# Bonus row sums in four column tiles, spread over partitions by a transfer through DRAM, and one weight tile's low part written in two halves

## The reference, cut to what matters

```
z = h @ w_in[l]
...
bonus = jnp.sum(rh * kh * r_k.astype(f32), axis=-1, keepdims=True) * vh
y = (y + bonus.reshape(B, T, RWKV_DIM)) * g.astype(f32)
```

## Time and profile before

| | us |
|---|---|
| median of 3 runs | 1086.53 (1085.99 to 1086.6) |
| the profiled execution | 1085.98 |
| its span, first to last instruction | 1084.4 |
| TensorE (PE) busy | 1068.5 |
| VectorE (DVE) busy | 670.7 |
| ScalarE (ACT) busy | 535.0 |
| GpSimd (POOL) busy | 109.3 |

### The profile page before, as it was taken

The page is one execution under the profiler, slowest core; times in us unless marked ns, Lnnn a source line. Parts: engine busy times, 40 slices in busy tenths (PEclk is TensorE's granted clock), DMA queues, the critical chain, the costliest instruction groups (busy, mean ns, idle before and its releaser), DMA issues.

```text
span 1084.4 us, 17833 instructions
## 1 busy us (share of the span) xinstructions
PE 1068.5 (99%) x6584; PEld 856.5 (79%) x6584; DVE 670.7 (62%) x1159; ACT 535.0 (49%) x1060; POOL 109.3 (10%) x164
## 2 busy tenths in 40 slices
PE   8999999999999999999999999999999999999997
PEld 7887888767787787787877888888888888888886
DVE  4224655687887887878765445557677777742124
ACT  6426675635545555555554334555555556531122
POOL 8100000220120220212110010100000000000000
PEclk9999999999999999999999999999999999999999
DMA  7633333321220312314133453423333332322221
GB/s 199 156 89 88 92 85 86 92 60 40 50 49 31 88 44 66 69 60 122 55 118 99 141 151 113 136 79 97 96 97 97 97 96 79 99 95 97 97 78 77
DMA packets 155190, 99.16 MB, mean 91 GB/s; under 512 B 31033, under 2 KB 143975, under 8 KB 155127
## 3 DMA queue, kind: packets, MB, share of 16 engines
q1 hardware_dynamic: 148800, 79.72, 25.5%
q0 software_dynamic: 6176, 18.53, 7.0%
q10 hardware_dynamic: 151, 0.04, 0.0%
HBM read 89.81 MB, written 8.45 MB: 91 GB/s over the span
## 4 chain that ended last, share of the span: by engine, by line
PE 95%; DVE 2%; ACT 1%; issue 1%; DMA 1%; SPq 0%; DVEq 0%; ACTq 0%
PE ps L1711 16%; PE ps L1714 16%; PE ps L1713 16%; PE ps L1667 5%; PE ps L1669 4%; PE ps L1668 4%; PE ps L2196 4%; PE ps L2197 4%; PE ps L2195 4%; PE ps L1829 3%; PE ps L1785 1%; PE ps L1981 1%; PE ps L1909 1%; PE ps L1960 1%; PE ps L1954 1%; PE ps L1886 1%
## 5 line engine op out<-in xcount | busy, mean ns | idle before, releaser
L1152 DVE TENSOR_TENSOR wlo<-raw,whi 128x1024 fp32r<-128x1024 f32 x142 | 173.7, 1223 | 213.6 <-ACT whi L729 141.5
L729 ACT ACTIVATE whi<-raw 128x1024 fp32r<-128x1024 f32 x124 | 131.1, 1057 | 124.6 <-PE ps L1714 120.8
L1711 PE MATMUL ps<-xnh,whi 128*128 128x512 f32 x344 | 135.8, 395 | 0.0
L1714 PE MATMUL ps<-xnh,wlo 128*128 128x512 f32 x344 | 135.7, 395 | 0.0
L1713 PE MATMUL ps<-xnl,whi 128*128 128x512 f32 x344 | 135.7, 395 | 0.0
L1711 PE MATMUL ps<-xh,whi 128*128 128x512 f32 x248 | 99.7, 402 | 1.5 <-DVE xl L1170 1.5
L1714 PE MATMUL ps<-xh,wlo 128*128 128x512 f32 x248 | 97.9, 395 | 0.0
L1713 PE MATMUL ps<-xl,whi 128*128 128x512 f32 x248 | 97.8, 395 | 0.0
L1667 PE MATMUL ps<-xh,whi 128*128 128x512 f32 x184 | 87.4, 475 | 0.4 <-DVE wlo L1152 0.4
L1711 PEld LDWEIGHTS ps<-xnh,whi 128*128 128x128 f32 x344 | 64.8, 188 | 15.2
L1713 PEld LDWEIGHTS ps<-xnl,whi 128*128 128x128 f32 x344 | 64.8, 188 | 15.1
(11 more groups left out here) (345 smaller groups left out, 2238.0 us busy)
## 6 DMA issues: line engine op xcount, KB each, us to landing
raw<-in_w_in SPq DMA_DIRECT2D x108, 256.0 KB, 3.3
raw<-in_w_up SPq DMA_DIRECT2D x88, 256.0 KB, 3.2
raw<-in_w_down SPq DMA_DIRECT2D x44, 256.0 KB, 2.9
gates_scratch<-gst POOLq DMA_DIRECT2D x16, 256.0 KB, 2.6
raw<-in_w_proj_b SPq DMA_DIRECT2D x16, 256.0 KB, 4.1
raw<-in_w_proj_a SPq DMA_DIRECT2D x16, 256.0 KB, 3.2
gl<-gates_scratch POOLq DMA_DIRECT2D x16, 256.0 KB, 3.1
raw<-in_w_out SPq DMA_DIRECT2D x16, 256.0 KB, 3.1
```

The source lines that it names most:

```text
L729: act.activation(flat(whi[:, hb]), flat(raw[:, b]), ACT.Copy).then_inc(w_hi, 1)
L1152: dve.tensor_tensor(flat(lo[:, hb]), flat(raw[:, b]), flat(hi[:, hb]).bitcast(F32), ALU.subtract).then_inc(w_lo, 1)
L1711: pe.matmul(ps[bank][:, :], whi[:, hb, k, :], hi(k), start=first and k == 0, stop=False)
L1714: ins = pe.matmul(ps[bank][:, :], wlo[:, hb, k, :], hi(k), start=False, stop=last and k == kn - 1)
```

## The change

1. `bonus` becomes `bonus_rows` for pairs 0 to 6: four products with 32 stationary columns (`rkcols`: the two head columns scaled by r_k) and 128 moving columns each, writing four groups of 32 partitions of bank 5. ScalarE copies the 128x128 result to `brow` between `ktok`'s copy and the turned output's (`bonus_sums`), and makes `rkcols` (128x32) in place of `rkones` (128x128).
2. GpSimd, behind `remainder(n)` and ahead of `key_norms_in(n+1)`, stores `brow` to DRAM, waits for that to land, and issues two transfers that read one row for each head back into 64 partitions of `z[:, d+8]` (`bonus_back`).
3. VectorE's `add_bonus` waits for these transfers and multiplies two tiles of SBUF; it moves from behind level 2 to behind level 3, and `with_bonus` from behind level 3 to behind level 5, ahead of `gated`.
4. The low part of weight tile 3n+1 was written at the start of `invert`, in one instruction. It is now written in two halves, behind level 1 and behind level 2. TensorE waits for the first half ahead of the tile's k = 0 and for the second ahead of k = 4.

```diff
@@ gpsimd
+            def bonus_back(d):
+                pool.wait_ge(brow_ready, d + 1)
+                pool.dma_start(bonus_rows, brow[:, :]).then_inc(brow_stored, 16)
+                pool.wait_ge(brow_stored, 16 * (d + 1))
+                for h in range(2):
+                    pool.dma_start(z[h * HD:(h + 1) * HD, d + 8, :]
+                                   .rearrange("p (j t) -> p j t", j=NT),
+                                   by_head(bonus_rows, h)).then_inc(bonus_in, 16)
...
                 remainder(n)
+                bonus_back(n - 1)
                 if n < PAIRS - 1:
                     pool.wait_ge(yturn_ps, n)
                     key_norms_in(n + 1)
@@ scalar
+            def bonus_sums(d):
+                act.wait_ge(bsum_ps, d + 1)
+                act.activation(brow[:, :], ps[5][:, 0:P], ACT.Copy).then_inc(brow_ready, 1)
...
                     if lv == 2:
-                        act.activation(rkones[:, :], headones[:, :], ACT.Copy, scale=pcol("rk", n))\
+                        dst, src = (rkcols, keycols[:, KEY0:KEY0 + P // NT]) if following else \
+                            (rkones, headones[:, :])
+                        act.activation(dst[:, :], src, ACT.Copy, scale=pcol("rk", n))\
...
                 token_copies(n)
+                bonus_sums(n - 1)
                 turned_output(n - 1)
@@ vector
             def add_bonus(d):
-                dve.wait_ge(bonus_ps, d + 1)
-                dst, bank = (tile(d + 8), 5) if d < PAIRS - 1 else (bp[:, :], 2)
-                chain(dve.tensor_tensor(dst, tile(d + 16), ps[bank][:, :], ALU.mult))
+                if d < PAIRS - 1:
+                    dve.wait_ge(bonus_in, 32 * (d + 1))
+                    chain(dve.tensor_tensor(tile(d + 8), tile(d + 16), tile(d + 8), ALU.mult))
...
+            def weights_half(n, half):
+                ks = slice(half * KT // 2, (half + 1) * KT // 2)
+                if half == 0:
+                    dve.wait_ge(w_hi, n + 1)
+                last = dve.tensor_tensor(flat(wlo[:, n % HL, ks]), flat(raw[:, n % RAW, ks]),
+                                         flat(whi[:, n % HL, ks]).bitcast(F32), ALU.subtract)
+                last.then_inc((w_half, w_lo)[half], 1)
...
-                if d is not None:
-                    weights(N_FILL + 3 * n + 1)
...
-                    if lv == 2 and d is not None:
-                        add_bonus(d)
-                    if lv == 3 and d is not None:
-                        with_bonus(d)
+                    if lv in (1, 2) and d is not None:
+                        weights_half(N_FILL + 3 * n + 1, lv - 1)
                     if lv == 3:
+                        if d is not None:
+                            add_bonus(d)
                         fill_low(3 * n)
                     if lv == 4:
                         weights(N_FILL + 3 * n + 2)
                     if lv == 5 and d is not None:
+                        with_bonus(d)
                         gated(d)
@@ tensor
                         k = self.k
+                        if k == 0 and self.half:
+                            pe.wait_ge(w_half, self.half)
+                        if k == (KT // 2 if self.half else 0):
+                            pe.wait_ge(w_lo, n + 1)
                         if k == 0:
-                            pe.wait_ge(w_lo, n + 1)
                             pe.wait_ge(ps_free, self.free)
...
+            def bonus_rows(d):
+                pe.wait_ge(rk_product, d + 1)
+                pe.wait_ge(rk_ready, d + 1)
+                for j in range(NT):
+                    r = j * (P // NT)
+                    ins = pe.matmul(ps[5][r:r + P // NT, 0:C], rkcols[:, :],
+                                    z[:, d + 8, j * C:(j + 1) * C], start=True, stop=True)
+                ins.then_inc(bsum_ps, 1)
```

More of the change, by code:

```diff
@@ L236, in build @@
         rkones = take("rkones", [P, P])
+        brow = take("brow", [P, P])
         take = taker(KVR, PREP)
@@ L242, in build @@
         gk = take("gk", [P, NT, 2, 2 * C])
+        rkcols = take("rkcols", [P, P // NT])
         yah = at(XHL, "yah", [P, KT, T], F32R)
@@ L274, in build @@
         key_rows = nc.dram_tensor("key_scratch", (P, P), F32, kind="Internal").ap()
+        bonus_rows = nc.dram_tensor("bonus_scratch", (P, P), F32, kind="Internal").ap()
         ps = [ctx.enter_context(nc.psum_tensor(f"ps{b}", [P, T], F32)) for b in range(8)]
@@ L280, in build @@
         w_hi = sem("w_hi")
+        w_half = sem("w_half")
         w_lo = sem("w_lo")
@@ L332, in build @@
         kqn_in = sem("kqn_in")
+        bsum_ps = sem("bsum_ps")
+        brow_ready = sem("brow_ready")
+        brow_stored = sem("brow_stored")
+        bonus_in = sem("bonus_in")
         tanh_ready = sem("tanh_ready")
@@ L1037, in _ @@
             act.wait_ge(q_back[3], 16)
-            act.wait_ge(bonus_ps, PAIRS)
+            act.wait_ge(bonus_ps, 1)
             act.wait_ge(pair_done, PAIRS - 1)
@@ L1323, in add_bonus @@
             def add_bonus(d):
-                dve.wait_ge(bonus_ps, d + 1)
-                dst, bank = (tile(d + 8), 5) if d < PAIRS - 1 else (bp[:, :], 2)
-                chain(dve.tensor_tensor(dst, tile(d + 16), ps[bank][:, :], ALU.mult))
+                if d < PAIRS - 1:
+                    dve.wait_ge(bonus_in, 32 * (d + 1))
+                    chain(dve.tensor_tensor(tile(d + 8), tile(d + 16), tile(d + 8), ALU.mult))
+                else:
+                    dve.wait_ge(bonus_ps, 1)
+                    chain(dve.tensor_tensor(bp[:, :], tile(d + 16), ps[2][:, :], ALU.mult))
             def with_bonus(d):
@@ L1653, in _, with __init__ @@
             class Tile:
-                def __init__(self, n, bank, hi, lo, free):
+                def __init__(self, n, bank, hi, lo, free, half=None):
                     self.n, self.bank, self.hi, self.lo, self.free, self.k = n, bank, hi, lo, free, 0
+                    self.half = half
                 def __call__(self, count):
@@ L1845, in scores @@
                 if d is not None:
-                    bonus(d)
+                    bonus_rows(d)
             def invert(n, d, following, fill):
@@ L2030, in following @@
                         free = N_FILL + (t, t - 2, t - 1)[t % 3] if t else N_FILL - 2
-                        self.tile = Tile(N_FILL + t, FILL_BANK[t % 3], xs(xh), xs(xl), free)
+                        self.tile = Tile(N_FILL + t, FILL_BANK[t % 3], xs(xh), xs(xl), free,
+                                         t // 3 if t % 3 == 1 else None)
                     else:
```

## The result

The changed kernel takes 1088.08 us (median of 20 runs, 1086.75 to 1090.11), the kernel before 1086.28 us beside it (20 runs, 1085.73 to 1087.97). The ratio is 1.0014 with an interval of 1.0008 to 1.0021: about 1.5 us slower by the ratio and 1.8 by the medians, 0.14% to 0.17%. The profiled execution took 1088.41 us with a span of 1086.8, where the one before had 1084.4.

What follows compares the result with a forecast made beforehand. TensorE's own work was taken as the bound (95% of the chain). Terms -2.2 - 1.0 - 0.6 + 4.8 = +1.0 us gave 1087.0 profiled, plus 0.55 for the median of runs: 1087.5, range 1082.7 to 1090.0.

Steps and rivals of the forecast that it cites:

- The likeliest case: Forecast as summed, gains and the level 6 loss together: 1086.5 to 1088.5 us, chance 0.53.
- the sum: All terms, -2.2 - 1.0 - 0.6 + 4.8 = +1.0 us, on the profiled execution of 1085.98 us: 1087.0.
- The tiles, -2.2: Bonus product on TensorE as column tiles: 0.89 instead of 1.20, saving 0.31 in each of 7 pairs, 2.2 us.
- The low part leaves the start, -1.0: Without the subtraction at the start of `invert`, level 1's 0.15 hole on TensorE goes in seven stages: 1.0 us saved.
- The halves, -0.6 and 0: Behind level 2, level 3's 0.12 hole closes in five pairs, 0.6 saved; behind level 1, just in time, no cost.
- Level 6, +4.8: `with_bonus` ahead of `gated` delays VectorE's `v` pair: 0.71 lost in pairs 1 to 6, 0.50 in pair 7.
- The transfers, 0: Detour through DRAM: reads land at 412.5, needed at 413.27, 0.75 slack, cost 0; upper bound about 1.5 each, 11.
- free tile switches: Rival: entering and leaving the tiled form costs nothing, saving 4.5 instead of 2.2; total -1.3, 1085.2 us; chance 0.12.
- the cover at level 6: Rival: the added 0.72 on VectorE finds cover, so the gains stand alone: -3.8, 1082.7 us; chance 0.18.

Runs made afterwards that it cites:

- the second kernel: Changed kernel with the four column-tile products replaced by one full-width product of 128 stationary by 512 moving columns: 1089.94 us, ratio 1.0030.
- the fourth kernel: Changed kernel without the store to DRAM and the reads back, VectorE waiting for ScalarE's copy only: 1087.78 us, ratio 1.0010.
- the third kernel: Changed kernel with the low part of the weight tile written whole at the start of `invert`, as before the change: 1090.71 us, ratio 1.0033.
- the first: Changed kernel with the addition of the bonus product done by GpSimd instead of VectorE, `add_bonus`'s multiplication also losing its `chain`: 1082.54 us, ratio 0.9961.
- fifth: Changed kernel with both bonus instructions, multiplication and addition, on GpSimd behind the key norms' reads: 1081.22 us, ratio 0.9948 to the kernel before.
- eighth: Changed kernel with the key norms' two reads issued ahead of the bonus sums' two reads in GpSimd's queue: 1092.85 us, ratio 1.0058.
- the sixth: Kernel with both bonus instructions on GpSimd, its column-tile products split into two visits, two tiles ahead of the filler and two behind: 1084.14 us, ratio 0.9976.
- seventh: Kernel with both bonus instructions on GpSimd, all eight column-tile products written a second time in the same visit: 1083.24 us, ratio 0.9973.

## Why the prediction was right

The likeliest case came about: 1088.08 against 1087.5, within the range and within 0.2% of before. The profiled execution, 1088.41 against the 1087.0 that the sum gives, was further off, by pair 1's landing. The steps, one by one:

- **The tiles, -2.2.** Right, in the row (0.89) and in the time (the second kernel).
- **The low part leaves the start, -1.0.** Right: level 1's hole is gone, and with the subtraction put back it is 0.46, as the prediction's 0.15 and 0.31 add up to. It and the tiles belong together: alone, the tiles would have fed the hole.
- **The halves, -0.6 and 0.** Right in the rows: level 3 at 0.41, and level 2 just in time, also at 0.41; the gain of level 3 is lost at level 4 in pairs 1 and 2, as forecast. No run takes the halves alone, so their share of the time isn't shown.
- **Level 6, +4.8.** Right in place, mechanism and size. Only the shape of the row was foreseen wrongly: I expected one long row of 1.1, but the first half of `v` is late too, so the whole group starts 0.52 late and its second half 0.20 more.
- **The transfers, 0.** This is the term that was too low. In six of seven stages they cost nothing. In pair 1's the second read took 6.9 instead of the 5.0 that I took, and 1.2 of TensorE's time in the profiled execution. That is all of what the stages lose beyond the sum (2.23 against 1.0); without the transfers, in the fourth kernel, they lose 0.94. I had tied the longer landing to a weight load in flight. That doesn't carry it: here the load's first packet came when the read was overdue, and in the third kernel's trace the second reads of pairs 2, 4 and 5 had over 600 packets of a weight load beside them and took 4.9 to 5.1. The lateness isn't bound to pair 1 either. Its second read took 6.36, 5.97, 5.77, 6.16 and 5.77 in the traces of the first, second, third, fifth and eighth kernels, but 4.74 and 4.75 in the sixth's and seventh's, while pair 6's took 5.90 in the second's, pair 3's 5.69 in the third's and pair 4's 5.78 in the seventh's. In the changed kernel and the first, second, fifth and seventh, each read over 5.1 had a 16 KB packet of the instruction queue starting 3.5 to 3.9 behind its issue; the one read with such a packet near that place (3.35) that wasn't late is pair 7's in the seventh, behind which no other read is queued. But pair 3's in the third was late without such a packet. So this is a coincidence in rows, not tested, and the cause stays open. In the unprofiled runs the share may be smaller: the medians differ by 1.5 to 1.8, and the fourth kernel gained only 0.3.

By the Trainium skill, "DMA: Bandwidth & Descriptors", section on the anatomy of a transfer from GpSimd, a read would have taken an estimated 2.3 us (2.0 and 128 KB at 436 GB/s). The traces don't agree: 4.5 to 6.9.

Of the rivals, free tile switches are refuted by the second, sixth and seventh kernels, and the cover at level 6 by the first. On "TensorEngine Tiling (Array Packing)" of the Trainium skill, section "Tiling Modes", the drain on a change of mode agrees with the sixth and seventh kernels: 0.22 for a visit, with two tiles or four. The 0.33 by which the saving (0.31) fell short of a free switch (0.64) is more than this, because it also has the filler's first product: its step to the next is 0.34 instead of 0.23, and it is 0.31 to 0.32 behind small products that aren't tiled too (408.61 to 408.92 in the changed kernel's pair 4).

## What to carry to other kernels

Before an instruction is moved to another slot of a busy engine, look at the end of that slot: where two engines meet with no slack, its full step is added to the path, in each pass of the loop. Two edits that each look small can depend on each other, as the faster product did on the clearing of the wait behind it. An addition that fits no slot of VectorE may cost nothing on GpSimd at twice the duration, if its input is there early and its user late; and work in a tiled form belongs together in one visit.

## What the runs showed of the hardware that was not expected

- A visit to the 32-column form costs 0.44 us with two passes for each tile, whether two or four tiles are used; 0.22 of it are the passes, 0.22 coming and going.
- GpSimd's addition of two 128x512 float32 tiles took 1.28 us, VectorE's 0.68.
- VectorE's subtraction into a low part took 1.84 us once (284.84, fifth kernel) among 135, whose median is 1.226. It was the only one in the fifth kernel beside GpSimd's bonus addition, which had started first and ended at 284.32 + 1.28 = 285.60; from there to 286.68, the end of the subtraction, it is 1.08. So most of the subtraction ran only when GpSimd was done. Where VectorE starts first, GpSimd is held instead. Timeline of the changed kernel, GpSimd's product of r and k in the stages of pairs 0 and 1, and VectorE's subtraction beside the second:

```profile
225.65 1.28 POOL L644 TENSOR_TENSOR z<-z,kmod 128x512 f32<-128x512 f32 x1
...
265.14 1.22 DVE L1178 TENSOR_TENSOR wlo<-raw,whi 128x1024 fp32r<-128x1024 f32 x1
...
265.37 2.12 POOL L644 TENSOR_TENSOR z<-z,kmod 128x512 f32<-128x512 f32 x1 [33.87 <-DVE kp L1307]
```

  In all seven stages with a subtraction beside it, started 0.23 earlier, the product took 2.12, and the subtraction kept its 1.22. In pair 4's stage of the fifth kernel GpSimd's two instructions stood beside VectorE instructions that read PSUM, and these kept their 0.75 to 0.76. The Trainium skill says it in "SBUF — State Buffer", section "SBUF: two separate sides": VectorE with two SBUF inputs and GpSimd exclude each other for a whole instruction, and whichever starts first goes first. These rows agree, in both directions.
- A read from DRAM that is queued behind two others in GpSimd's queue was only issued later; in its own time from issue to landing (4.4 to 5.8 us, eighth kernel) the others didn't show.
